# A gated delta rule's inverse on Trainium2: its first five doubling levels as two 64x64 matmul tiles in opposite corners of the array

## The reference, cut to what matters

```python
lmat = jnp.where(pos[:, None] > pos[None, :],
                 jnp.einsum('nbhid,nbhjd->nbhij', kb, kc) * decay, 0.0)
rhs = jnp.concatenate([vc * bc[..., None], kb * jnp.exp(gc)[..., None]], axis=-1)
sol = lax.linalg.triangular_solve(lmat, rhs, left_side=True, lower=True, unit_diagonal=True)
...
def step(s, inp):
    v_new = u_i - jnp.einsum('bhcd,bhde->bhce', w_i, s)
    s_next = s * gl_i[..., None, None] + jnp.einsum('bhcd,bhce->bhde', kd_i, v_new)
```

## Time and profile before

| | us |
|---|---|
| median of 3 runs | 4983.92 (4981.96 to 4986.58) |
| the profiled execution's own time | 4974.38 |
| its span in the profile | 4972.6 |
| TensorE busy | 3731.7 (75%), granted clock 0.869 of full |
| VectorE (DVE), ScalarE (ACT), GpSimd (POOL) busy | 1310.5, 757.4, 887.8 |
| levels 0 to 4 of all twelve steps (six in each of two scans) | 363.73 |

### The profile page before, as it was taken

How to read it: one execution, slowest core, us unless ns; L and a number is a source line. 1 busy time by engine, 2 the same in 40 slices (tenths; PEclk the granted TensorE clock), 3 DMA queues, 4 the chain that set the end, 5 groups by cost and what they waited for, 6 DMA issues and landing times. The chain is left out here.

```text
span 4972.6 us, 54079 instructions
## 1 busy us (share of the span) xinstructions
PE 3731.7 (75%) x18691; PEld 2178.1 (44%) x18692; DVE 1310.5 (26%) x2238; ACT 757.4 (15%) x1472; POOL 887.8 (18%) x924
## 2 busy tenths in 40 slices
PE   7598998998657885898488875795758628888882
PEld 3358976895323332343233322351434315555541
DVE  0253444343310002212200002107444321111115
ACT  0142233221011111000011110010014001111110
POOL 0004421441021111000111110005200022222223
PEclk9698999999779998899599997898669769999996
DMA  6490000000259997612399996310010118997895
GB/s 238 123 221 1 1 18 34 1 1 35 73 231 410 404 395 318 232 51 89 128 402 392 405 374 244 130 60 17 1 62 1 49 65 287 336 318 270 306 334 185
DMA packets 214054, 900.21 MB, mean 181 GB/s; under 512 B 52962, under 2 KB 53860, under 8 KB 179748
## 3 DMA queue, kind: packets, MB, share of 16 engines
q1 hardware_dynamic: 165316, 805.05, 43.4%
q0 software_dynamic: 22368, 50.39, 3.3%
q10 hardware_dynamic: 26240, 43.01, 2.5%
HBM read 839.32 MB, written 78.46 MB: 185 GB/s over the span
## 5 line engine op out<-in xcount | busy, mean ns | idle before, releaser
L1430 PE MATMUL ps<-weight_ring,moe_xT 128*64 128x256 f32 (+1 forms) x1344 | 444.9, 486 | 71.3 <-issue 69.0
L1430 PE MATMUL ps<-moe_spare,moe_xT 128*64 128x256 f32 (+1 forms) x1280 | 422.8, 485 | 66.3 <-issue 66.3
L1432 PE MATMUL ps<-weight_ring,moe_xT 128*64 128x256 f32 (+1 forms) x1344 | 445.9, 487 | 0.0
L1432 PE MATMUL ps<-moe_spare,moe_xT 128*64 128x256 f32 (+1 forms) x1280 | 423.8, 485 | 0.0
L1404 POOL COPY moe_xg<-moe_xin 64x1024 f32<-64x1024 f32 x168 | 173.5, 1033 | 1287.3 <-PE ps L1418 668.6
L258 PE MATMUL ps<-weight_ring,mod_wide 128*128 128x512 f32 x640 | 289.7, 607 | 142.2 <-DVE mod_wide L241 133.0
L1513 DVE TENSOR_TENSOR moe_act<-moe_sg,ps 64x256 f32<-64x256 f32 (+1 forms) x164 | 87.2, 532 | 972.7 <-ACT moe_sg L1491 972.7
L1430 PEld LDWEIGHTS ps<-weight_ring,moe_xT 128*64 128x64 f32 x1344 | 188.0, 142 | 300.4 <-issue 269.0
L1430 PEld LDWEIGHTS ps<-moe_spare,moe_xT 128*64 128x64 f32 x1280 | 177.6, 141 | 286.6 <-issue 257.1
L1516 DVE COPY moe_y<-ps 128x512 f32 x164 | 113.4, 691 | 690.5 <-PE ps L1449 495.8
L1449 PE MATMUL ps<-weight_ring,moe_aT 128*64 128x512 f32 x944 | 241.1, 645 | 26.7 <-issue 16.6
(11 more groups left out here) (515 smaller groups left out, 5761.9 us busy)
## 6 DMA issues: line engine op xcount, KB each, us to landing
weight_ring<-in_w_dram SPq DMA_DIRECT2D x96, 2048.0 KB
moe_spare<-in_w_dram SPq DMA_DIRECT2D x96, 2048.0 KB
weight_ring<-in_w_exp_gu_dram SPq DMA_DIRECT2D x32, 2048.0 KB
moe_spare<-in_w_exp_gu_dram SPq DMA_DIRECT2D x32, 2048.0 KB
weight_ring<-in_ada_w_dram SPq DMA_DIRECT2D x24, 2048.0 KB
expert_rows<-moe_y ACTq DMA_DIRECT2D x328, 128.0 KB
weight_ring<-in_w_exp_dn_dram SPq DMA_DIRECT2D x16, 2048.0 KB
moe_spare<-in_w_exp_dn_dram SPq DMA_DIRECT2D x16, 2048.0 KB
```

Source lines behind the costliest of these rows:

```text
L1430: nc.tensor.matmul(m.ps[0:UR, 0, 0:F], xT[:, k, :], gate[:, k, :], start=(k == 0), stop=(k == KD - 1))
L1432: last = nc.tensor.matmul(m.ps[UR:P, 0, 0:F], xT[:, k, :], up[:, k, :], start=(k == 0), stop=(k == KD - 1))
```

## The change

In levels 0 to 4 no joined block is larger than 64 rows, so all that these levels compute lies in the upper left and the lower right 64x64 quarter of a head's 128x128 matrix. The change computes only these two quarters: each 128x128 product becomes two of 64x64, one on the array's rows and columns 0 to 63 and one on 64 to 127, half as many moving columns each (64 for Z, 32 for the corrections). Level 5 is as it was. DVE's subtractions also go by quarters, each as two instructions on 64 partitions. ACT's copy and POOL's masks keep their full size.

```diff
+    def quarter(ap, h, x):
+        return ap[64 * x:64 * x + 64, h * P + 64 * x:h * P + 64 * x + 64]
+
+    def quarters(ap, l, odd, x):
+        part = h3(ap)[64 * x:64 * x + 64, :, 64 * x:64 * x + 64]
+        return part.rearrange("p h (n two s) -> p h n two s", two=2, s=2 ** (l + 1))[:, :, :, int(odd), :]
...
                 for h in range(4):
-                    out, rhs = hd(bank(d, 0), h), hd(b["XT"], h)
                     if l == LV - 1:
-                        out, rhs = blocks(out, l, d == 0), blocks(rhs, l, d == 0)
-                    last = nc.tensor.matmul(out, hd(b["Tm"], h), rhs, start=True, stop=True)
+                        last = nc.tensor.matmul(blocks(hd(bank(d, 0), h), l, d == 0), hd(b["Tm"], h),
+                                                blocks(hd(b["XT"], h), l, d == 0), start=True, stop=True)
+                        continue
+                    for x in range(2):
+                        last = nc.tensor.matmul(quarter(bank(d, 0), h, x), quarter(b["Tm"], h, x),
+                                                quarter(b["XT"], h, x), start=True, stop=True)
...
+                    for h in range(4):
+                        for x in range(2):
+                            nc.tensor.matmul(blocks(quarter(bank(d, 1), h, x), l, d == 0), quarter(b["X"], h, x),
+                                             blocks(quarter(b["Z"], h, x), l, d == 0), start=True, stop=True)
+                    for h in range(4):
+                        for x in range(2):
+                            last = nc.tensor.matmul(blocks(quarter(bank(d, 2), h, x), l, d == 1), quarter(b["Z"], h, x),
+                                                    blocks(quarter(b["X"], h, x), l, d == 1), start=True, stop=True)
...
+                        for x in range(2):
+                            xt = quarters(b["XT"], l, d == 0, x)
+                            last = nc.vector.tensor_tensor(xt, xt, quarters(bank(d, 1), l, d == 0, x), ALU.subtract)
+                        last.then_inc(e.xt, 1)
+                        for x in range(2):
+                            xx = quarters(b["X"], l, d == 1, x)
+                            last = nc.vector.tensor_tensor(xx, xx, quarters(bank(d, 2), l, d == 1, x), ALU.subtract)
+                        last.then_inc(e.xx, 1)
```

More of the change, by code:

```diff
@@ L753, in level_pq @@
                     pe.wait_ge(e.attn, lat_count(i) + 1)
[L755 to L758, removed]
+                if l == XL:
                     for h in range(4):
-                        last = nc.tensor.matmul(blocks(hd(bank(d, 2), h), l, d == 1), hd(b["Z"], h),
-                                                blocks(hd(b["X"], h), l, d == 1), start=True, stop=True)
+                        last = nc.tensor.matmul(blocks(hd(bank(d, 1), h), l, d == 0), hd(b["X"], h),
+                                                blocks(hd(b["Z"], h), l, d == 0), start=True, stop=True)
+                else:
+                    for h in range(4):
[6 more added lines that the diff above has]
+                                                    blocks(quarter(b["X"], h, x), l, d == 1), start=True, stop=True)
                 last.then_inc(e.pq, 1)
@@ L947, in _ @@
                             dve.wait_ge(e.xx, XL * i + l)
[L948 to L953, removed]
+                        if l == XL:
+                            xt = blocks(b["XT"], l, d == 0)
+                            nc.vector.tensor_tensor(xt, xt, blocks(bank(d, 1), l, d == 0), ALU.subtract
+                                                    ).then_inc(e.xt, 1)
+                            continue
+                        for x in range(2):
[6 more added lines that the diff above has]
+                        last.then_inc(e.xx, 1)
                 for d in range(2):
```

## The result

The changed kernel takes 5001.18 us (median of 8 runs, 4995.46 to 5013.29) against 4982.36 us before (8 runs, 4974.95 to 4986.58): ratio 1.0042, interval [1.0031, 1.0054]. It is slower, by 18.8 us or 0.4%: little, but the interval leaves out 1. The forecast was 5009 us, 25 us slower, with slower as the likeliest side.

A forecast was written before the change was run, and what follows sets the result against it. TensorE was taken to bound levels 0 to 4, at a clock staying half: levels -34 and later work +60 give +26 on 4974.4, 5000; the median's 9.5 makes 5009 us. Likeliest range 4995 to 5030, full range 4865 to 5040.

The forecast's parts named there:

- The step on which all hung: Levels 0 to 4: the shorter z streams leave the granted clock at half throughout; chance 0.54.
- One reason given beside it: Levels 0 to 4: each record uses only half of the array's rows, given as support for the clock staying at half.
- The level at half: One changed level at the half clock: 5.29 us from z_f to z_f, level 0 6.2, level 4 5.4.
- The term -34 us: Levels 0 to 4 over twelve steps: 27.5 us a step against 30.31, so -2.8 a step.
- The tail: Level 5, make_w and onward to the next step: slower at half clock, +5 us a step, bounds +2 and +8.
- The term +60: Work behind levels 0 to 4, summed over twelve steps at +5 us each because the clock returns late.
- The overlap: Levels 0 to 4: matmuls on the two opposite corner tiles run at once, 0.054 us a record at half clock.
- Rows 7 and 8: Profile rows from attention scores and experts: matmuls on row halves and on column halves overlap; opposite corners appear in neither.
- streams in turn: Rival, levels 0 to 4: corner loads overlap but streams take turns in one PSUM bank; level 6.15 us, 5058 us, chance 0.05.
- The rival of no idle gaps: Levels 0 to 4: TensorE idle only 0.16 of 5.29 us, so the clock returns, with the time of the first rival.
- The level at the full clock: One changed level once the clock is full: 3.2 to 3.3 us against 5.42 before.
- the first rival: Clock comes back in level 0 or 1, making the kernel faster: 4868 us (4855 to 4880), chance 0.27.

The follow-up runs named there:

- corners for z alone: Changed kernel with only z as 64x64 corners, pq kept as the full 128x128 product: 5205.69 us in one run (4976.15 before).
- wide z: Changed kernel with z's corner matmuls streaming all 128 columns instead of 64, the added ones zeros: 4892.46 us, ratio 0.9823 to before.
- wide pq: Changed kernel with pq streaming 64 columns instead of 32, added ones zeros, and DVE's old subtractions: 4850.27 us; with the new subtractions 4862.92 us.
- streams ahead: Changed kernel with seven useless 512-column matmuls a step where TensorE would wait ahead of the levels: 4837.62 us, ratio 0.9724 to before.
- corners in sequence: Changed kernel with each group's four upper left corners first, then the four lower right ones: 5041.37 us in one run (4977.67 before).

## Why the prediction was right

**The clock.** The step on which all hung, that z with 64 columns between pq groups with 32 would not bring the clock back, held in all twelve steps. It is shown, not only argued: the same corners entered at full stay at full and gain 2.8%, and with more columns in z or in pq they find the full clock by themselves. That being occupied with weight loads doesn't raise the clock is shown too, by corners for z alone: loads in 26.03 of 26.62 us, at 0.50. One reason given beside it did not carry the result: each record uses only half of the rows in wide z and wide pq as well, and there the clock came back.

**The level at half.** Forecast 5.29 (level 0 6.2, level 4 5.4), measured 5.25 (6.23 and 5.39); 27.35 a step against 27.5. Each part of it fits: pq_f 1.87 behind z_f as forecast, pq 3.38 against 3.42. The term -34 us was -35.5.

**The tail.** Forecast +5 a step, bounds +2 and +8; measured +4.8, with the clock back 8.8 to 11.8 us behind z_f of level 5. The term +60 was +57. With the levels' -35.5 the two terms give +22 instead of +26, half of the 8 us by which 5009 was high. Another 1.6 is before's own median, which moved from 4983.92 to 4982.36 with more runs, and the rest lies within the spread of the runs.

**The overlap.** Rows 7 and 8 carried it rightly to opposite corners: 0.053 us a record. With streams in turn a level would be longer, and it is 5.25. The price of that rival was too low, though: it let pq_f start 2.73 us behind z_f, but z_b stands ahead of it in the queue, and two groups of 1.71 in turn end at 3.42. The level would be 3.42 + 3.42 = 6.84, not 6.15, and the time near 5095, not 5058. It had a chance of 0.05 and lay outside the range, so nothing else depends on it. The rule of "TensorEngine Tiling (Array Packing)" in the Trainium skill, Gotcha 1, that different row tiles can't access one PSUM bank at the same time, is not borne out here: the corners write different partitions of one bank, and a pair every 0.105 us is the pace of one tile.

**The rival of no idle gaps.** The advice of the Trainium skill, "TensorE: Matmul & The Clock Gate", closing table, that the prediction weighed would have had the clock back; 21.12 of 21.12 us busy at 0.50 differ from it, and 26.62 of 26.62 in the kernel with corners for z alone more so.

**What was mis-sized.** The level at the full clock, 3.2 to 3.3, is 3.59 in the changed kernel with streams ahead: DVE's two instructions were taken as 0.29 us overlapping by 0.08, 0.50 in all, and are 0.58, 0.62 from one pair to the next. I also looked for this only at z_f; the wait is z_b's. It touched the first rival's time alone: with three levels of 3.6 it would have been near 4880 instead of 4868.

**What stays open.** Why the return of the clock shifts between steps of one kernel was not tested. Nor was the number of columns of a record parted from how long the streams last: wide z doubles both, and in wide pq the clock came back with 64 columns a record in all groups. The rows alone are ruled out, as said above.

## What to carry to other kernels

Before shrinking a matmul, look at the granted clock in its stage and at what TensorE did before it rose; if it was this matmul's stream, the smaller one can cost more, behind the stage too, in work that was not touched. Where weight loads set the pace, as here with 64 columns of weights, more moving columns can be almost free and useless ones may pay: 64 instead of 32 was worth 2.6% here. And a part that is hidden in a long level, like DVE's subtractions, has to be priced again when the level gets shorter.

## What had not been expected of the hardware

- More work in the same loops, all of it zeros, made the kernel faster: doubling z's columns by 2.2% and doubling pq's by 2.6% against after (ratios 0.9823 and 0.9779, by 1.0042).
- At the full clock the four pq groups of a level take 1.87 us with 32 columns (567.44 to 569.31) and 1.92 with 64 (519.27 to 521.19), so the added columns ride along almost free; with 128 in z a level is 3.99 instead of 3.59.
- By the trace, matmuls of different tiles pass each other in the queue: 5.95 us a level with the corners in sequence instead of the 10 or so expected if one tile waits for the other.
- A DVE instruction of 128 elements takes 0.29 us on 64 partitions as on 128, and one of 256 elements on 128 partitions 0.42. So halving the partitions gains nothing, and two instructions of 128 elements are 0.58.
